# Order of the products in the scores of a forgetting attention: mask first and grouped, or block by block with the mask last

## The reference, cut to what matters

```python
for i in range(S // Q_BLOCK):                 # 4 blocks of 128 queries
    q0 = i * Q_BLOCK
    kl = q0 + Q_BLOCK
    logits = jnp.einsum("bqhd,bkhd->bhqk", q[:, q0:kl], k[:, :kl]) * scale
    logits = logits + cum[:, :, q0:kl, None] - cum[:, :, None, :kl]
    mask = k_pos[None, :] <= q_pos[:, None]
    p = jax.nn.softmax(jnp.where(mask, logits, NEG_INF), axis=-1)
    outs.append(jnp.einsum("bhqk,bkhd->bqhd", p, v[:, :kl]))
```

## Time and profile before

| | |
|---|---|
| median of 3 runs | 2149.82 us (2148.6 to 2149.96) |
| profiled execution | 2149.96 us, its span 2147.8 us |
| PE busy | 96% of the span |
| DVE, ACT, POOL busy | 61%, 39%, 44% |
| from 196 to 311.6 us | PE busy 103.0 of 115.6 us, DVE 91.0, mean granted clock 0.82 |

### The profile page before, as it was taken

One profiled execution on the slowest core, in us unless ns is written; L12 is line 12 of the kernel. 1 busy time (PEld: TensorE's weight loads), 2 busy tenths in 40 slices (PEclk: granted clock), 3 DMA queues, 4 the chain that ended last, 5 costly groups with the idle time before them and its releaser, 6 DMA issues.

```text
span 2147.8 us, 23762 instructions
## 1 busy us (share of the span) xinstructions
PE 2058.3 (96%) x9763; PEld 1697.0 (79%) x9763; DVE 1304.7 (61%) x1650; ACT 838.1 (39%) x1207; POOL 937.2 (44%) x403
## 2 busy tenths in 40 slices
PE   7999989899999999999999999999998899999997
PEld 5778768778888887787888888887887788888886
DVE  7766971753235444564377776446669757777644
ACT  4633564651122224676343333224322234333322
POOL 4253146563444446112434444444667544444443
PEclk9999869999999999999999999999999999999999
DMA  6322102212222221111222222224222312222221
GB/s 200 147 105 79 59 20 99 78 59 96 92 93 92 98 98 67 35 48 60 79 79 98 98 93 87 98 77 167 99 88 98 110 68 81 96 98 98 98 98 40
DMA packets 34416, 191.96 MB, mean 89 GB/s; under 512 B 3887, under 2 KB 4479, under 8 KB 14916
## 3 DMA queue, kind: packets, MB, share of 16 engines
q1 hardware_dynamic: 34308, 190.44, 25.5%
HBM read 176.72 MB, written 13.64 MB: 89 GB/s over the span
## 4 chain that ended last, share of the span: by engine, by line
PE 83%; DVE 11%; ACT 3%; POOL 1%; issue 1%; DMA 0%; SPq 0%; ACTq 0%; DVEq 0%; POOLq 0%
PE ps L138 77%; PE ps L137 4%; DVE ps L173 1%; DVE X L161 1%; DVE X L173 1%; DVE VG L161 1%; PE ps L146 1%; DVE TMP L161 1%; DVE SM L182 1%; POOL WL L161 1%; DVE VG L173 0%; POOL X L161 0%; DVE QL L161 0%; DVE Y L161 0%; DVE HYL L161 0%
## 5 line engine op out<-in xcount | busy, mean ns | idle before, releaser
L161 POOL TENSOR_TENSOR WL<-W,WH 128x2048 fp32r<-128x2048 f32 (+3 forms) x157 | 663.6, 4229 | 950.5 <-ACT WH L154 947.0
L138 PE MATMUL ps<-HH,WL 128*128 128x512 f32 (+1 forms) x1408 | 545.8, 388 | 18.1 <-DVE HL L173 7.9
L138 PE MATMUL ps<-HH,WH 128*128 128x512 f32 (+1 forms) x1408 | 538.6, 383 | 0.0
L138 PE MATMUL ps<-HL,WH 128*128 128x512 f32 (+1 forms) x1408 | 538.5, 382 | 0.0
L154 ACT ACTIVATE WH<-W 128x2048 fp32r<-128x2048 f32 (+2 forms) x148 | 275.2, 1859 | 327.2 <-PE ps L138 327.2
L138 PEld LDWEIGHTS ps<-HH,WL 128*128 128x128 f32 x1408 | 265.3, 188 | 79.4 <-DVE HL L173 12.0
L138 PEld LDWEIGHTS ps<-HH,WH 128*128 128x128 f32 x1408 | 265.0, 188 | 51.7
L138 PEld LDWEIGHTS ps<-HL,WH 128*128 128x128 f32 x1408 | 265.5, 189 | 50.2 <-issue 0.2
L161 DVE TENSOR_TENSOR MRL<-MID,MRH 128x512 fp32r<-128x512 f32 x76 | 177.4, 2366 | 162.3 <-ACT MRH L154 162.3
L138 PE MATMUL ps<-MRH,WL 128*128 128x512 f32 x608 | 238.1, 392 | 3.3 <-ACT PAD L154 2.2
L138 PE MATMUL ps<-MRH,WH 128*128 128x512 f32 x608 | 236.7, 389 | 0.0
(11 more groups left out here) (357 smaller groups left out, 3315.9 us busy)
## 6 DMA issues: line engine op xcount, KB each, us to landing
W<-in_up SPq DMA_DIRECT2D x44, 1024.0 KB, 4.8
W<-in_down SPq DMA_DIRECT2D x22, 1024.0 KB, 4.8
W<-in_w_up SPq DMA_DIRECT2D x16, 1024.0 KB, 4.8
W<-in_w_down SPq DMA_DIRECT2D x16, 1024.0 KB, 4.8
W<-in_hy_in SPq DMA_DIRECT2D x12, 1024.0 KB, 4.8
kd<-STG SPq DMA_DIRECT2D x36, 256.0 KB, 2.0
KB<-kd SPq DMA_DIRECT2D x8, 1024.0 KB, 5.4
W<-in_win_ag SPq DMA_DIRECT2D x4, 1024.0 KB, 4.9
```

What stands on the lines that cost most here:

```text
L138: return self.eng.matmul(out, lhs, rhs, start=start, stop=stop)
L161: return QUIET if self.eng is None else self.eng.tensor_tensor(out, a, b, op)
```

## The change

`fox_s` is written in another order. Before: the banks of all blocks are opened, then come the four mask products, the twelve 64-row products of the four blocks, and the four 4-row products. After: block by block, the bank is opened, and then come its three 64-row products, its 4-row product, and its mask product, which now ends the block and raises the event. Number and sizes of the products are the same, 20 for a head. The first product of a block now starts the accumulation of its bank's region.

```diff
             def fox_s(h):
                 pb, j, ab, g = 64 * (h % 2), h // 2, 32 * (h % 4), h // 4
-                hd = slice(pb, pb + 64)
-                for i in (0, 2, 3):
-                    open_bank("fs", h, max(i, 1))
                 for i in range(4):
                     nk = 128 * (i + 1)
-                    pe.mm(logits(h, i)[:, nk - 128:nk], IDR[:], MKR[:], i != 1, False, True)
-                pe.wait_ge(*at("q", j))
-                pe.wait_ge(*at("k", j))
-                for i in range(4):
-                    nk = 128 * (i + 1)
-                    pe.mm3(logits(h, i), QH[hd, j, blk(i)], QL[hd, j, blk(i)], KH[hd, j, 0:nk], KL[hd, j, 0:nk],
-                           False, False, True)
-                for q in range(4):
-                    pe.wait_ge(*at("aug", q, g))
-                for i in range(4):
-                    ins = pe.mm(logits(h, i), QA[ab:ab + 4, g, blk(i)], KA[ab:ab + 4, g, 0:128 * (i + 1)], False, True,
-                                True)
+                    if i != 1:
+                        open_bank("fs", h, max(i, 1))
+                    ps = logits(h, i)
+                    qs, hd = blk(i), slice(pb, pb + 64)
+                    pe.wait_ge(*at("q", j))
+                    pe.wait_ge(*at("k", j))
+                    pe.mm3(ps, QH[hd, j, qs], QL[hd, j, qs], KH[hd, j, 0:nk], KL[hd, j, 0:nk], True, False)
+                    for q in range(4):
+                        pe.wait_ge(*at("aug", q, g))
+                    pe.mm(ps, QA[ab:ab + 4, g, qs], KA[ab:ab + 4, g, 0:nk], False, False)
+                    ins = pe.mm(ps[:, nk - 128:nk], IDR[:], MKR[:], False, True)
                     if i:
                         ins.then_inc(*up(acc, ("fs", h, i)))
```

## The result

The changed kernel took 2163.62 us, median of 4 runs (2162.15 to 2164.11), beside 2149.21 for the kernel before: ratio 1.0058, 95% interval 1.0044 to 1.0073. All eleven executions of it in this measurement lie from 2156.01 to 2164.11, with a median of 2161.53, and the ratio fits this better than 2163.62. Measured again later (e5) it took 2159.73, median of 6 (2154.75 to 2164.01): 1.0048, interval 1.0031 to 1.0064. It is slower by 10 to 14 us. The forecast was 2154.9 with a range to 2160.0: the direction was right, the size too small. The later median lies just inside the range, the first one outside.

A forecast was written before the change was run, and what follows sets the result against it. PE, busy 96% of the span, was taken to pace the kernel. S(5) 5.5 us later became 5.0 at head 5's maxima, then -0.4 and +0.5: +5.1 on 2149.82 gives 2154.9 us, range 2146.5 to 2160.

The forecast's parts named there:

- The price of a change of the row count: PE's score groups: 9 more changes a head at 0.14 us each, growing a group from 3.51 to 4.81 us.
- The front: S(0) to S(1): S(0) grows 1.3, one low-clock stretch costs 1.7, T(0) hides 1.0; S(1) starts 2.0 us later.
- The rounds: PE's heads 1 to 4: 13.33 us plus 1.25 low-clock stretches makes 15.4 each, four 61.6; S(5) starts 5.5 later.
- rival 3: PE's rounds: two low-clock stretches each, 16.7 us, some +10; held as the forecast range's far end, no separate chance.
- From S(5) to the memory's keys: Head 5 onward: shorter delay to the end of the maxima, DVE's wait for S(6) gone, S(7) grown; sum +5.1.
- The 7.3 down to 6.8 of the maxima: Head 5 on DVE: maxima end 6.8 us after S(5) starts instead of 7.3, so 5.0 later than before.
- the -0.4: DVE's wait of 0.39 us for S(6) goes, as three of its blocks need no bank of DVE's work.
- the +0.5: S(7), partly at low clock, adds 0.5 us, chosen between nothing and the 1.3 of its growth.
- Rival 1: Attention rounds: clock falls no more often, DVE paces and its waits go; -2.8 us, 2147.0, or -4.1; chance 0.17.
- Rival 2: Low stretches only at the front and over S(7), rounds between fit DVE's; 0 to +3, say 2151.3 us; chance 0.23.
- Rival 4: Products on different row groups overlap in four heads, groups there grow 0.4; some -3, 2146.8 us; chance 0.05.

The follow-up runs named there:

- e5: The changed kernel measured again, unedited, for its interval and a second trace: 2159.73 us, ratio 1.0048.
- e1: Changed kernel with products grouped by row count again, banks still opened one by one and masks last: 2149.35 us, ratio 0.9994.
- e3: Changed kernel, order by blocks kept, all score products over 128 rows instead of 64 and 4 (other scores): 2144.36 us, ratio 0.9966.
- e4: Kernel before, grouped order kept, all score products over 128 rows (other scores): 2147.99 us, ratio 0.9990.
- e2: Changed kernel with all three banks opened ahead of the first block, as before: 2160.82 us, ratio 1.0045.
- e6: Changed kernel with the 4-row product taken over the head's 64 rows, 8 changes of row count in a head: 2150.72 us, ratio 1.0004.
- e11: Changed kernel with the 4-row product taken over 32 rows, 28 of them zeros, same output: 2156.19 us, ratio 1.0033.
- e13: Grouped order (3 changes) with six 128x512 products over 128 rows added ahead of each group: 2151.25 us, ratio 1.0013.
- e14: Grouped order (3 changes) with block 3's 4-row product made seven times instead of once: 2157.40 us, ratio 1.0046.
- e8: Changed kernel with its 64-row products over 128 rows, 4-row product left, 8 changes in a head: 2146.75 us, ratio 0.9988.
- e9: Changed kernel with two full 128x512 products added ahead of block 2 and two ahead of block 3: 2163.88 us, ratio 1.0061.

## Why the prediction was wrong

**The price of a change of the row count** was right but for 0.1 us a group: 0.14 for each, a group of 4.81 us; measured 4.91, which is 0.16 for each of the nine.

**The front** was right in the first trace. From the start of S(0) to that of S(1) it had 2.0 us more. Measured 13.2 (199.2 to 212.4) instead of 11.06 (197.04 to 208.10): 2.2 more, with a low stretch of 3.4 us from 203.8 on, over the end of S(0) and QK(3). In e5 the low stretch was 6.8 us and the front 14.75, 3.7 more than before.

**The rounds** are the step that failed: "With 1.25 low stretches to a round, 2.1, it is 15.4". From S(1) to S(5) the first trace has 23.9 us of low clock, 1.75 stretches of 3.41 to a round, the second 27.3, 2.0. Four rounds took 65.0 us (212.4 to 277.4) and 66.5, not 61.6. That is 3.4 to 4.9 us too little in one term. The mechanism was the one forecast, and the mis-sized term is the 1.25: it measured 1.75 and 2.0. The arithmetic holds with the measured number: 13.33 + 1.75 x 1.7 = 16.3, measured 16.25.

Why nearly two: the number had been chosen between one and two, with the groups of before in mind, where S(1) and S(4) had no fall. But once PE is the pace all rounds are nearly alike. In each of them the clock fell late in the group by blocks or just behind it, and the low stretch went on over PV, in most rounds into QK. I had this as "rival 3", priced it at some +10, and cut the range at 2160 by "a few that escape it". In e5 none escaped. That the median of e5 lies just inside the range doesn't mend the term.

**From S(5) to the memory's keys** (the first product on `HM`): 44.2 us (277.4 to 321.6), before 45.4 (266.2 to 311.6). The 7.3 down to 6.8 of the maxima, the -0.4 and the +0.5 make -0.4 together, where -1.2 was measured: 0.8 too high.

**In sum** the stage from S(0) to `HM` grew from 114.6 us to 122.4 in the first trace and 125.4 in e5: +7.8 and +10.8, where +5.1 was forecast. The terms account for it: 0.2 and 1.7 too little at the front, 3.4 and 4.9 in the rounds, 0.8 too much behind S(5). In the first trace there are 2.2 us more ahead of S(0) and 1.6 behind the start of `HM`. Neither belongs to the change with any surety: S(0) starts between 196.4 and 200.3 us in the traces of all versions, whose code is the same up to there, and from the first product on `HM` to the end it is 1836.2 and 1834.7 us in the two traces before, 1837.8 and 1837.5 in the changed kernel, 1838.2 in e1. What of the 14.4 us between the first medians is more than the 11.6 between the two spans is not located. The second pair, 9.8 us, is of the size of the stage's growth.

**Rival 1** (the pipelining wins) has something to it and lost: e3 against e4 shows a gain of 3.6 us for the order, of which the traces place 1.2 in this stage, and e2 shows that the late opening is worth nothing when PE is the pace. **Rival 2** needed rounds that fit under DVE's; at 8 changes (e6) its time is about what was measured. **Rival 4**'s working has a slip: with groups 0.9 us shorter PE's rounds are 12.4 in half of the heads, and 12.9 is the mean of all. It is out in any case: a group of e11 takes 4.94 us in head 0, where the rows of the running sums (32 there) lie among the head's 64, and 4.91 in head 1, where they don't.

**The causes, by what was shown.** That giving up the grouping by row count is all of the loss: e1 keeps the late opening and the late mask and has no loss, e2 lacks the late opening and has the whole. That what fills the added time decides how often the clock falls: e13 and e14 have equal changes and equal length, e14 costs 6.2 us more, and its rounds look like those of the changed kernel. e8 against e6 points the same way in the clock (1.00 against 0.91), and hardly in the time of the stage. That length and low clock work together: PE becomes the pace of every round in e14, and not in e13, which costs 1.9 us over e1. How the loss of the changed kernel divides is argued and not shown. By e13 the length would be the smaller part, but e13's length is made of full products, which may hold the clock up. What stays open too is why filling inside the group (e9) didn't help, and how the 2 to 6 us between e14 and the changed kernel come about.

## What to carry to other kernels

Group small products by their row count, and count the changes of it, some 0.16 us each at 2.4 GHz here (4.91 against 3.51 us for nine more). Before trusting an order that starts work earlier, work out the round of each engine with the new length; a gain that comes from filling an engine's waits is gone once that engine is the pace. If PE then runs without a gap through products with few rows, take a low stretch in every round as the forecast and not as the far end: here it was 23.9 and 27.3 us out of four rounds of 65.0 and 66.5.

## What was not expected of the hardware

The granted clock fell from 2.4 to 1.2 GHz in rounds in which PE had no idle time at all: three times between 231 and 266 us in the changed kernel, in each case after 3.6 to 4.5 us of a score group, whose products are mostly over 64 and 4 rows. With the 64-row products widened to 128 (e8) the groups S(0) to S(4), 4.4 to 4.5 us of products each, ran through at 2.4 GHz. With the 4-row products widened to 64 instead (e6), two falls came in the same rounds, at 212.5 and 226.1.
